# Long convolution: a GpSimd fold moved ahead of a low part, and two magnitude tiles added before the column sum

## The chip, the cores and the metric

One core of one Trainium2 chip (trn2) runs the whole program. The metric is device time in microseconds of that core; what is given is the median of three runs, and one more execution was profiled. Inputs, outputs and all arithmetic are fp32; most matmuls run on fp32r pairs, a high part and a low part.

## The reference, cut to what matters

The program is two blocks of a language model, one after the other. The change lies in the first mixer of the first block, a long convolution over T = 528 positions and E = 2048 channels. Its filters come from a small network, are weighted by a decay, and are divided by the sum of their magnitudes:

```python
filt = (hdn @ w4.astype(F32)).reshape(T, 2, D_INNER)
filt = filt * jnp.exp(-t * deltas[None, :])[:, None, :]
filt = filt / (jnp.sum(jnp.abs(filt), axis=(0, 1), keepdims=True) + HY_FILTER_EPS)
...
y = jnp.fft.irfft(jnp.fft.rfft(vf, n=n, axis=1) * jnp.fft.rfft(taps, n=n, axis=0)[None], n=n, axis=1)[:, :T]
return (y + vf * skip.astype(F32)).astype(v.dtype)
```

What the change touches is the sum of magnitudes over positions, one number for each channel, and the order of work around it.

## The kernel before, in words

The five engines (TensorE, ScalarE, VectorE, GpSimd, called POOL, and SyncE) each run a program written out by hand, and wait for each other by counters ("cv.pe", "cv.vec", "cv.act", "cv.pool"). Nothing is planned by a scheduler: the order on each engine is the order in the functions `tensor_conv`, `scalar_conv`, `vector_conv`, `gpsimd_conv` and `sync_conv`.

The 2048 channels are cut into 8 chunks c of 256, each two halves h of 128. The Fourier transforms are matmuls with tables. Positions are folded first (sum and difference of a position and its mirror), which leaves 265 rows in three tiles: 128, 128 and 9 (the 9 repeated, 41 partitions). Frequencies come in five groups z: two even, two odd, and a rest. In chunk c, each group z goes like this:

- TensorE: `tensor_freq` part 0, the transform of the signal (14 passes), then `tensor_filter`, a step of the filter network's last layer for chunk c+1, then `tensor_freq` part 1, the transform of the filter. Behind group 1 it transposes the folded signal of chunk c+1, half 0, and behind group 3 half 1 (`tensor_turned`, L1095, six transposes, three for each of two folds m).
- ScalarE: `scalar_freq` evicts the filter's part (hc), `scalar_filter` takes magnitudes for chunk c+1, `scalar_product` rounds the product's high part into Y_h.
- VectorE: `vector_filter` multiplies taps and decay into hp (L1007), `vector_differ` forms sums and differences into fsum (L1023, two instructions), `vector_freq` multiplies signal and filter (L1196, from PSUM) and forms real and imaginary parts rr (L1202, L1203). `vector_larger` (L1029) takes the larger of two magnitudes: with a = forward plus backward and b = forward minus backward, |forward| + |backward| = max(|a|, |b|), so the tile dec[:, i] then holds magnitudes, for i in the three tiles of positions and s in two parts of 256 channels.
- POOL: `gpsimd_freq` makes the low part Y_l of the product (L103). Behind group 1 of chunk c it folds half 1 of chunk c+1 (`gpsimd_fold`: for each of two folds m an add or subtract of 128x263 at L1077 and two small copies at L1078 and L1080). Behind groups 0 and 1 it also makes the low part of the finished output y of chunk c-1 (`gpsimd_out`). Behind group 4 come the low part of the next weights (`gpsimd_w4`), the fold of half 0 for chunk c+2, and two products of gate and signal (`gpsimd_back`, L1275).

Then TensorE transforms back (`tensor_back`, 48 passes; `tensor_back_end`, L1231, 8 passes, which wait for POOL's low part of group 4), and `tensor_filter_end` (L1056) sums the magnitudes of chunk c+1 over positions: for each half h six matmuls with one column on the moving side, dec as the weights, against ones, or against wf[:, 6] (2 in partition 0, 1 elsewhere, since position 0 stands in halved) for the first tile, or against wf[:, 5] (1 for the nine true rows) for the third. The hardware runs an fp32 matmul of this kind as two passes, so the 12 matmuls are 24 passes of LDWEIGHTS and MATMUL. VectorE reads the sums (`vector_filter_end`), adds 1e-6 and takes the reciprocal rn, which scales the output of chunk c+1 at its end.

Behind the mark "norm" of `tensor_filter_end`, SyncE loads the next chunk's decay into dec (`sync_conv`). After "norm" TensorE starts chunk c+1 with `tensor_freq`, whose bank must be free of VectorE's read y0 (`vector_back`, L1259 and L1260, first half).

In chunk 0 part of this work stands ahead, inside the projections of the mixer: POOL issues the tables' loads (L1443 to L1445), makes the low part of the weights of chunk 1 (`gpsimd_w4(e, w, 1)`), waits for the projections to be over (`hyena_over`), issues one more table and folds half 0 of chunk 1. TensorE runs `tensor_filter_end` for chunk 0 after the signal's transform of groups 0 and 1. Chunk 7 has no filter work.

Of the kernel before, what the change touches and what calls it, by code (L numbers as in the profile page):

```python
# [6 lines left out]
F32 = mybir.dt.float32  # L7
# [3 lines left out]
ALU = mybir.AluOpType  # L11
# [129 lines left out]
def build(nc, stack, I, C, out):  # L141
# [3 lines left out]
    def sb(name, shape, dt, at):  # L145
        return nc.alloc_sbuf_tensor_at(name, shape, dt, offset=at, align_bytes=16)
# [220 lines left out]
    HT = at  # L367
# [209 lines left out]
    def sync_norm0(e, w):  # L577
# [14 lines left out]
                      for j, n in enumerate("hl"))  # L592
    wf = sb("wf", [128, 7], F32, HT + 16704)
    w4r = sb("w4r", [128, 2, 256], F32, PH2)
# [436 lines left out]
    def scalar_filter(e, w, c, step):  # L1031
# [14 lines left out]
        act(e, abs0[0:n], hp[0:n, 0, :], ACT.Abs).then_inc(*mark("cv.act", "abs0", c, i))  # L1046

    def tensor_filter_end(e, w, c):
        w.wait_ge("cv.vec", "vT", c, 0)
        w.wait_ge("wf")  # L1050
        once, first_ = wf[:, 5:6], wf[:, 6:7]
        for h in range(2):
            for i in range(3):
                w.wait_ge("cv.vec", "ab", c, i)
                for s in range(2):
                    t = e.matmul(vb[0][:, h:h + 1], lhsT=dec[:, i, s, 128 * h:128 * h + 128], rhs=once if i == 2 else first_ if i + s == 0 else ones[:, 0:1],  # L1056
                                 start=(i == 0 and s == 0), stop=(i == 2 and s == 1))
        t.then_inc(*mark("cv.pe", "norm", c))
# [367 lines left out]
    def gpsimd_conv(e, w):  # L1426
# [17 lines left out]
        e.dma_start(flat(lf[0][:]), C["lf"][0]).then_inc(*land("mats2"))  # L1444
        e.dma_start(lb_x[:], C["lb"]).then_inc(*land("mats2"))  # L1445
        gpsimd_w4(e, w, 1)
        hyena_over(w)
# [5 lines left out]
        for c in range(8):  # L1453
            for z in range(5):
                gpsimd_freq(e, w, c, z)
                if c < 7 and z == 1:
                    gpsimd_fold(e, w, c + 1, 1)
                if c and z < 2:
                    gpsimd_out(e, w, c - 1, z)
            if c < 6:  # L1460
                gpsimd_w4(e, w, c + 2)
                gpsimd_fold(e, w, c + 2, 0)
            if c < 7:
                gpsimd_back(e, w, c, 0)
                gpsimd_back(e, w, c, 1)
# [2885 lines left out]
def constants():  # L4351
# [26 lines left out]
    co[264] = 0  # L4378
    wf = np.full((128, 7), 2 / 1056, np.float32)
    wf[:, 5] = np.arange(128) < 9  # L4380
    wf[:, 6] = 1
    wf[0, 6] = 2
    wf[0, 0] = 1 / 1056
# [81 lines left out]
```

## Time and profile before

| | |
|---|---|
| median of three runs | 2385.81 us (2380.79 to 2391.12) |
| profiled execution, its own time | 2386.13 us |
| its span | 2384.2 us |
| busy in the span: TensorE / its weight loads | 2226.8 us (93%) / 1848.7 us (78%) |
| VectorE / ScalarE / POOL | 1365.9 (57%) / 1002.5 (42%) / 623.7 (26%) |
| mean granted TensorE clock | 0.969 of full speed |
| the convolution's main loop | about 416 to 704 us of the span |

Times on the traces are microseconds from the span's start. The profiled execution's own time is the span and 1.9 us around it. A timeline row gives start, length, engine, line, operation, the tile written and the tiles read; "x2" means that two like instructions are merged, and their length is from the first's start to the last's end. In brackets stands the idle time before it and what ended it. An instruction's length on VectorE and POOL includes the time for which it was issued and stood still. The lines L99, L103 and L115 are helpers (high part, low part, activation), so tiles tell them apart.

### The profile page before, as it was taken

Reading aid. Unit: us, or ns where it says so; the run is one execution under the profiler, and the core shown is the slowest. Engines: PE = TensorE matmul, PEld = TensorE weight load, DVE = VectorE, ACT = ScalarE, POOL = GpSimd, SP = SyncE. Lnnn points to the kernel's source line nnn. Section 1 sums busy time; section 2 is a strip of 40 time slices with the busy share of each in tenths; the row PEclk is TensorE's granted clock in tenths of the full one; section 3 lists DMA queues with packets and bytes.
Section 4 is the critical chain, followed back from the end, with each engine's and each line's share of the span. In section 5 each row is a group of like instructions: output and inputs, shape, how many; then the busy total and the mean of one; then the engine's idle time right before and its main releaser. Section 6 shows DMA issues by size and latency. Waiting matters only on the chain.

```text
span 2384.2 us, 36903 instructions
## 1 busy us (share of the span) xinstructions
PE 2226.8 (93%) x15305; PEld 1848.7 (78%) x15305; DVE 1365.9 (57%) x2335; ACT 1002.5 (42%) x1824; POOL 623.7 (26%) x520
## 2 busy tenths in 40 slices
PE   7999999999999899999999989889989999699997
PEld 7999999899999888999999967856776677333332
DVE  4455545898863566667666666789455664411112
ACT  4434434444442455655656552435424432211112
POOL 1111123555631122322322201203220111133331
PEclk9999999999999999999999989999988999799999
DMA  5322332210033222322222224312331143799993
GB/s 183 96 82 89 93 114 64 72 36 19 32 104 95 72 64 73 82 69 72 80 68 75 54 53 118 89 36 76 95 106 49 32 146 98 291 363 374 375 374 145
DMA packets 228641, 274.78 MB, mean 115 GB/s; under 512 B 41448, under 2 KB 193993, under 8 KB 215930
## 3 DMA queue, kind: packets, MB, share of 16 engines
q1 hardware_dynamic: 212634, 256.68, 33.7%
q0 software_dynamic: 15264, 13.65, 1.8%
q8 instruction: 121, 1.98, 0.3%
q10 hardware_dynamic: 576, 2.10, 0.2%
q14 instruction: 46, 0.38, 0.0%
HBM read 305.18 MB, written 23.13 MB: 138 GB/s over the span
## 4 chain that ended last, share of the span: by engine, by line
PE 69%; DVE 15%; ACT 8%; issue 3%; POOL 2%; DMA 1%; SPq 0%; ACTq 0%; POOLq 0%; DVEq 0%
PE ps L93 15%; PE ps L94 15%; PE ps L95 15%; PE ps L4065 7%; PE ps L4108 4%; ACT sp L115 2%; ACT whi L99 2%; DVE wlo L103 2%; PE ps L1876 2%; PE ps L4035 1%; DVE p L2174 1%; PE ps L3181 1%; PE ps L3126 1%; PE ps L1056 1%; PE ps L3048 1%
## 5 line engine op out<-in xcount | busy, mean ns | idle before, releaser
L93 PE MATMUL ps<-hn_h,whi 128*128 128x264 f32 (+2 forms) x2256 | 688.9, 305 | 27.2 <-DVE wlo L103 8.5
L94 PE MATMUL ps<-hn_l,whi 128*128 128x264 f32 (+2 forms) x2256 | 670.4, 297 | 0.0
L95 PE MATMUL ps<-hn_h,wlo 128*128 128x264 f32 (+2 forms) x2256 | 670.3, 297 | 0.0
L93 PEld LDWEIGHTS ps<-hn_h,whi 128*128 128x128 f32 x2256 | 429.6, 190 | 52.7 <-issue 19.2
L94 PEld LDWEIGHTS ps<-hn_l,whi 128*128 128x128 f32 x2256 | 430.1, 191 | 9.6 <-issue 0.2
L95 PEld LDWEIGHTS ps<-hn_h,wlo 128*128 128x128 f32 x2256 | 428.6, 190 | 11.5
L103 POOL TENSOR_TENSOR wlo<-wraw,whi 128x2048 fp32r<-128x2048 f32 (+1 forms) x44 | 158.4, 3601 | 465.8 <-ACT whi L99 465.8
L99 ACT ACTIVATE whi<-wraw 128x2048 fp32r<-128x2048 f32 (+1 forms) x134 | 202.4, 1511 | 44.1 <-PE ps L95 37.9
L103 DVE TENSOR_TENSOR wlo<-wraw,whi 128x2048 fp32r<-128x2048 f32 (+1 forms) x90 | 172.0, 1911 | 50.4 <-ACT whi L99 50.2
L4065 PE MATMUL ps<-ex_raw,xT 128*64 128x512 f32 x600 | 135.4, 595 | 0.0
L766 DVE SCALAR_TENSOR_TENSOR c<-ub,vec,c 128x528 f32<-128x528 f32 x48 | 45.5, 948 | 123.3 <-ACT c L115 123.3
L4079 DVE SCALAR_TENSOR_TENSOR gt<-gt,ps 128x256 f32<-128x256 f32 x24 | 10.1, 421 | 171.4 <-ACT gt L115 171.4
L4065 PEld LDWEIGHTS ps<-ex_raw,xT 128*64 128x64 f32 x600 | 42.0, 137 | 76.4 <-issue 74.2
L115 ACT ACTIVATE ub<-ps,vec 128x528 f32<-128x528 f32 x48 | 33.7, 702 | 143.0 <-PE ps L95 143.0
L115 ACT ACTIVATE p<-ps,stat 128x528 f32<-128x528 f32 x64 | 45.0, 703 | 106.4 <-DVE stat L2160 106.4
L4108 PE MATMUL ps<-ex_raw,aT 128*64 128x512 f32 x312 | 87.6, 598 | 0.5 <-ACT aT L115 0.5
L2160 DVE TENSOR_REDUCE stat<-ps 128x1 f32<-128x528 f32 x128 | 84.0, 697 | 2.3 <-PE ps L1876 1.3
L115 ACT ACTIVATE gt<-ps 128x256 f32<-128x256 f32 x24 | 9.2, 384 | 161.3 <-PE ps L4065 161.3
L93 PE MATMUL ps<-yh,whi 128*128 128x272 f32 (+1 forms) x256 | 73.8, 288 | 2.4 <-POOL yl L103 2.4
L94 PE MATMUL ps<-yl,whi 128*128 128x272 f32 (+1 forms) x256 | 73.5, 287 | 0.0
L95 PE MATMUL ps<-yh,wlo 128*128 128x272 f32 (+1 forms) x256 | 73.4, 287 | 0.0
L2174 DVE SCALAR_TENSOR_TENSOR p<-p,stat,sp 128x528 f32<-128x528 f32 x60 | 46.1, 768 | 47.5 <-ACT sp L115 47.5
(703 smaller groups left out, 5296.8 us busy)
## 6 DMA issues: line engine op xcount, KB each, us to landing
ex_raw<-in_w_gate_up SPq DMA_DIRECT2D x49, 1024.0 KB, 7.8
wraw<-in_hy_w_in SPq DMA_DIRECT2D x32, 1024.0 KB, 5.7
wraw<-in_da_w_in SPq DMA_DIRECT2D x64, 512.0 KB, 4.2
ex_raw<-in_w_down SPq DMA_DIRECT2D x26, 1024.0 KB, 7.7
wraw<-in_w_gate_up SPq DMA_DIRECT2D x15, 1024.0 KB, 7.6
wraw<-in_w_in SPq DMA_DIRECT2D x14, 1024.0 KB, 5.4
wraw<-in_hy_w_out SPq DMA_DIRECT2D x8, 1024.0 KB, 7.6
wraw<-in_da_w_out SPq DMA_DIRECT2D x8, 1024.0 KB, 7.7
```

The lines of the kernel that those rows point to most:

```text
L93: e.matmul(out, lhsT=l[0], rhs=r[0], start=start, stop=False)
L94: e.matmul(out, lhsT=l[0], rhs=r[1], start=False, stop=False)
L95: return e.matmul(out, lhsT=l[1], rhs=r[0], start=False, stop=stop)
L99: return e.activation(hi, src, ACT.Copy, bias=0.0, scale=scale)
L103: return e.tensor_tensor(lo, src, hi.bitcast(F32), ALU.subtract)
L115: return e.activation(out, in_, func, bias=bias, scale=scale, accum_out=accum)
L766: e.scalar_tensor_tensor(cc[:], u[:, 0:T], V["conv_w0"][:, q:q + 1], cc[:], ALU.mult, ALU.add).then_inc(*mark("hy.vec", "tap", x))
L1876: t = e.matmul(sc[m][:, y, 0:264], lhsT=qk[l][c, q], rhs=qk[r][c, ks], start=(l + r == 0), stop=(l == 1))
L2160: e.tensor_reduce(mx[:, m:m + 1], sc[m][:, :, 0:264], AX.XY, ALU.max, negate=True).then_inc(*mark("da.vec", "max", h, i, m))
L2174: e.scalar_tensor_tensor(p[0][:], p[0][:], ls[:, 0:1], p[1][:], ALU.mult, ALU.add).then_inc(*mark("da.vec", "p", h, i))
L4065: t = e.matmul(bank[2 + n % 2][half, :], lhsT=xT[n % 2][:, 4 * g + k, half], rhs=unsplit(c)[:, k, :], start=(g == 0 and k == 0), stop=(g = ...
L4108: t = e.matmul(bank[6 + g][half, :], lhsT=aT[n % 2][:, k, half], rhs=unsplit(c)[:, k, 512 * g:512 * g + 512], start=(k == 0), stop=(k == 1))
```

## The change

Three things change. POOL folds half 1 of chunk c+1 ahead of the low part of group 1 instead of behind it; the low part of y stays behind. POOL adds the first magnitude tile onto the second (128x512) and then the second's two channel parts together (128x256), in a new function `gpsimd_total`, which stands ahead of the low part of group 4 for chunk c+1, and for chunk 0 behind the tables' loads. And `tensor_filter_end` runs, for each half, four matmuls for six: the sum tile against ones, one partition (position 0) once more against one, which takes the place of the weight 2, and the two of the third tile. These are 16 passes for 24. It now waits for POOL's total and for the last maximum before its first pass. The column wf[:, 6] goes.

```diff
+    def gpsimd_total(e, w, c):
+
+        w.wait_ge("cv.vec", "ab", c, 1)
+        a, b = (dec[:, i].rearrange("p s c -> p (s c)") for i in range(2))
+        e.tensor_tensor(b, b, a, ALU.add).then_inc(*mark("cv.pool", "both", c))
+        w.wait_ge("cv.pool", "both", c)
+        e.tensor_tensor(dec[:, 1, 0], dec[:, 1, 0], dec[:, 1, 1], ALU.add).then_inc(*mark("cv.pool", "total", c))
+
     def tensor_filter_end(e, w, c):
         w.wait_ge("cv.vec", "vT", c, 0)
         w.wait_ge("wf")
-        once, first_ = wf[:, 5:6], wf[:, 6:7]
+        once = wf[:, 5:6]
+        w.wait_ge("cv.pool", "total", c)
+        w.wait_ge("cv.vec", "ab", c, 2)
         for h in range(2):
-            for i in range(3):
-                w.wait_ge("cv.vec", "ab", c, i)
-                for s in range(2):
-                    t = e.matmul(vb[0][:, h:h + 1], lhsT=dec[:, i, s, 128 * h:128 * h + 128], rhs=once if i == 2 else first_ if i + s == 0 else ones[:, 0:1],
-                                 start=(i == 0 and s == 0), stop=(i == 2 and s == 1))
+            out, cols = vb[0][:, h:h + 1], slice(128 * h, 128 * h + 128)
+            e.matmul(out, lhsT=dec[:, 1, 0, cols], rhs=ones[:, 0:1], start=True, stop=False)
+            e.matmul(out, lhsT=dec[0:1, 0, 0, cols], rhs=ones[0:1, 0:1], start=False, stop=False)
+            for s in range(2):
+                t = e.matmul(out, lhsT=dec[:, 2, s, cols], rhs=once, start=False, stop=s == 1)
         t.then_inc(*mark("cv.pe", "norm", c))
...
         e.dma_start(lb_x[:], C["lb"]).then_inc(*land("mats2"))
+        gpsimd_total(e, w, 0)
         gpsimd_w4(e, w, 1)
         hyena_over(w)
...
         for c in range(8):
             for z in range(5):
-                gpsimd_freq(e, w, c, z)
                 if c < 7 and z == 1:
                     gpsimd_fold(e, w, c + 1, 1)
+                if c < 7 and z == 4:
+                    gpsimd_total(e, w, c + 1)
+                gpsimd_freq(e, w, c, z)
                 if c and z < 2:
                     gpsimd_out(e, w, c - 1, z)
```

## Rows read from the trace of the kernel before

**Rows 1.** Busy by stretch: length, PE, PEld, DVE, ACT, POOL busy, clock, DMA share, GB/s.
```profile
450.00:485.00 35.00, 32.95 (x275) 32.24 (x273) 32.27 (x48) 16.84 (x28) 21.10 (x22) 1.00 0.10 31
```

**Rows 2.** Chain of waits in order of time: start, length, what.
```profile
416.15 2.59 PE ps L1056 x24
...
450.30 2.57 PE ps L1056 x24
...
519.90 2.57 PE ps L1056 x24
...
555.78 3.01 PE ps L1056 x24
...
593.22 2.90 PE ps L1056 x24
...
666.56 2.57 PE ps L1056 x24
```

**Rows 3.** Waits, 415 to 705 us: total us, times, longest.
```profile
PEld ps L1095 <- POOL fold L1080: 10.8, 7, 1.6
...
PE ps L1095 <- POOL fold L1080: 9.0, 7, 1.4
```

**Rows 4.** Timelines, TensorE and weight load, chunk 1: start, length, engine, line, operation.
```profile
469.87 0.54 PE L1095 MATMUL ps<-ident,fold 128*128 128x128 f32 x3
...
471.79 0.29 PEld L1095 LDWEIGHTS ps<-ident,fold 128*128 128x128 f32 x3 [1.64 <-POOL fold L1080]
```

**Rows 5.** Timeline of VectorE, chunk 1.
```profile
457.53 1.23 DVE L1196 TENSOR_TENSOR prods<-ps,hc 128x1024 f32<-128x1024 f32 x1 [0.20 <-ACT hc L115]
...
461.04 3.41 DVE L1023 TENSOR_TENSOR fsum<-hp 128x512 f32<-128x512 f32 x2
...
465.62 0.42 DVE L1202 TENSOR_TENSOR rr<-prods 128x256 f32<-128x256 f32 x1
...
468.92 0.50 DVE L1202 TENSOR_TENSOR rr<-prods 128x256 f32<-128x256 f32 x1
...
470.38 1.29 DVE L1023 TENSOR_TENSOR fsum<-hp 128x512 f32<-128x512 f32 x2
472.84 0.68 DVE L1007 TENSOR_TENSOR hp<-ps,dec 41x512 f32<-41x512 f32 x1 [1.17 <-PE ps L988]
...
475.37 0.69 DVE L1029 TENSOR_TENSOR dec<-dec,sq 128x512 f32<-128x512 f32 x1
...
477.54 1.29 DVE L1023 TENSOR_TENSOR fsum<-hp 41x512 f32<-41x512 f32 x2
```

**Rows 6.** Timeline of GpSimd (POOL), chunk 1.
```profile
460.70 1.47 POOL L103 TENSOR_TENSOR Y_l<-rr,Y_h 128x512 fp32r<-128x512 f32 x1 [1.36 <-ACT Y_h L99]
462.12 1.78 POOL L103 TENSOR_TENSOR yl<-gg,yh 128x528 fp32r<-128x528 f32 x1
...
468.38 0.76 POOL L1077 TENSOR_TENSOR fold<-vv 128x263 f32<-128x263 f32 x1
...
471.69 1.31 POOL L103 TENSOR_TENSOR yl<-gg,yh 128x528 fp32r<-128x528 f32 x1
472.97 1.29 POOL L103 TENSOR_TENSOR Y_l<-rr,Y_h 128x512 fp32r<-128x512 f32 x1
476.19 1.29 POOL L103 TENSOR_TENSOR Y_l<-rr,Y_h 128x512 fp32r<-128x512 f32 x1 [1.93 <-ACT Y_h L99]
481.68 1.29 POOL L103 TENSOR_TENSOR Y_h<-rr,Y_h 17x512 fp32r<-17x512 f32 x1 [4.19 <-ACT Y_h L99]
```

**Rows 7.** Timeline of ScalarE, chunk 1.
```profile
469.78 0.63 ACT L99 ACTIVATE Y_h<-rr 128x512 fp32r<-128x512 f32 x1 [1.53 <-DVE rr L1203]
```

**Rows 8.** Timelines of GpSimd and VectorE, chunk 0.
```profile
414.32 0.57 POOL L1445 DMA_DIRECT2D lb_x<-c_lb  x1
...
423.00 0.69 DVE L1007 TENSOR_TENSOR hp<-ps,dec 128x512 f32<-128x512 f32 x1 [0.96 <-DMA dec<-c_dec]
```

**Rows 9.** Busy by stretch, behind the passes at 519.90.
```profile
523.00:527.00 4.00, 4.00 (x24) 4.00 (x23) 3.88 (x7) 0.00 (x0) 3.88 (x7) 0.58 0.75 228
```

More of the change, by code:

```diff
@@ L592, in build @@
                       for j, n in enumerate("hl"))
-    wf = sb("wf", [128, 7], F32, HT + 16704)
+    wf = sb("wf", [128, 6], F32, HT + 16704)
     w4r = sb("w4r", [128, 2, 256], F32, PH2)
@@ L4378, in constants @@
     co[264] = 0
-    wf = np.full((128, 7), 2 / 1056, np.float32)
+    wf = np.full((128, 6), 2 / 1056, np.float32)
     wf[:, 5] = np.arange(128) < 9
-    wf[:, 6] = 1
-    wf[0, 6] = 2
     wf[0, 0] = 1 / 1056
```

## The prediction

> **What bounds the kernel now.** I read busy time by stretch first. In the stretch that holds chunk 1 of the convolution, TensorE is busy 32.95 of 35 us and VectorE 32.27, so two engines are almost full and neither can be shortened alone [rows 1]. GpSimd has 21.10 us of work. Next the chain of waits in order of time, for its marks: the 24 passes that sum the magnitudes start at 450.30, 519.90, 555.78, 593.22 and 666.56 us (the blocks near 485.1 and 630.7 are not shown), so chunks 1 and 2 take 69.60 us, 34.8 each, chunk 3 35.88, chunk 4 37.44, and the six periods 216.26 together, 7.46 more than six of 34.8 [rows 2]. The extra lies in chunks 3 to 6, at the lower clock, below. Then who waits for whom: TensorE and its weight load wait for the fold's last copy in seven chunks, 9.0 and 10.8 us in all [rows 3]. The timelines of TensorE and of its weight load show it once: three transposes at 469.87, and the weight load for the next three at 471.79, idle 1.64 us before it until the fold ended [rows 4].
>
> **The change, TensorE's part.** Per chunk 24 passes become 16. The 24 take 2.57 us, 0.107 us a pass [rows 2]. Eight fewer: 0.86 us a chunk. Four of the sixteen read one partition of dec; no row has such a pass. From below I bound it by nothing, from above by 0.107 us; I take 0.107, since they load the same 128 columns. The range that this leaves is 0.43 us a chunk, 3 us in all. The Trainium skill ("TensorE: Matmul & The Clock Gate", section "LDWEIGHTS (loading the stationary operand)") says that a load costs by its columns and not by the rows in contraction, which is also 0.107 here; no run here shows it. With the fold ahead of the low part of group one, the 1.64 us go as well: POOL ends the first low part of y at 463.90, what the fold waits for (the transposes of the first half, ahead of group two) is over by then, and two adds of 0.75 with four small copies end near 467.7, two us before TensorE asks [rows 4, 6]. Together TensorE could run 2.5 us a chunk faster, if nothing else stopped it.
>
> **VectorE's part.** It gets back what it waited for TensorE: 1.17 us before hp at 472.84, and 0.20 us before the products at 457.53 [rows 5]. That is 1.37 us a chunk; with this alone its period is 33.4 us, over TensorE's 32.3. So VectorE sets the pace, and what delays VectorE counts in full.
>
> **What delays VectorE.** Two sums of L1023 take 1.29 us for the pair at 470.38, but 3.41 us at 461.04 [rows 5]. In the second case POOL ran a low part (460.70 to 462.17) and another (462.12 to 463.90, 1.78 us where the same kind took 1.31 at 471.69) [rows 6]. The times fit a strict alternation: the sum waits for POOL's instruction, POOL's next waits for the sum, and so on, 2.1 us lost for VectorE. The product at 457.53 reads PSUM and takes 1.23 us; such instructions I count as free of it. So the position of every POOL instruction against VectorE's SBUF-only ones is a cost, and the change moves or adds ten of them a chunk (six of the fold, two low parts, two adds). By place:
> (a) The fold's adds now fall on 464 to 467, with the real and imaginary parts of group one (465.62, one of the two of 0.42) [rows 5]. At most one 0.75 us add stands in the way; I take 0.3, least 0.
> (b) The second low part of y (1.31 us) leaves 471.69, where VectorE idled, and follows Y_l of group one at about 468.5 to 469.8, onto the real part at 468.92 [rows 5, 6]. Between 0 and 1.3; I take 0.5, where the add there now costs 0.08 (0.50 for 0.42).
> (c) Y_l of group two waits for folds until 472.97 now, though ScalarE wrote its high part at 469.78 to 470.41 [rows 6, 7]. It will start at once, between the two sums of L1023 at 470.38. Between 0 and 1.29; I take 1.05, the middle of the pattern at 461.04.
> (d) The new adds: 128x512, priced by the low part of the same shape (1.29 us), and 128x256, priced by the fold's add of 128x263 (0.76 us, 468.38) [rows 6]. They stand behind Y_l of group three, which ends at 477.48, and its input (the maximum, done at 476.06) is there. VectorE starts two sums at 477.54 [rows 5]. 0.06 us decides who is first. Between 0 and 2.04; I take 1.3, the first add in the way and the second partly.
> Sum (a) to (d): 3.15, less 1.37 is +1.8 us a chunk. The Trainium skill ("SBUF — State Buffer", section "SBUF: two separate sides") states this as a rule: GpSimd and a VectorE instruction with two SBUF inputs hold one shared pair of ports for a whole instruction and the other side blocks fully. By that, the sum would be the same; the 3.41 us pair agrees with it.
> Behind (d) the cost is not hidden: the last group's products, ScalarE's high part, POOL's low part of group four and TensorE's eight passes of L1231 follow in a chain, and before the change that low part is ready at 482.97, 1.1 us ahead of them (they take the last 1.0 us before the block at 485.1) [rows 6].
>
> **The queues.** total for chunk c+1 stands ahead of the low part of group four, which arrives 4.19 us after POOL went idle [rows 6]; that gap holds the 2.0 us. The 16 passes wait for total, done near 481, against 485 when TensorE arrives: nothing. SyncE's loads of the next dec wait for the passes, which are no later: nothing. For chunk 0 it is otherwise: total(0) comes behind the last table's load (414.32, done issuing at 414.89) [rows 8], takes 2.0 to 2.1, so until 417.0; the passes that started at 416.15 start then and end at 418.8 for 418.7 [rows 2]. The dec load behind them, for which VectorE waits 0.96 us at 423.00 [rows 8], slips with it, and the w4 low part on POOL moves to 418.3, still before TensorE. +0.1 us.
>
> **The clock.** The mean granted clock is 0.58 from 523 to 527 us, part of it at the lower level, 1.2 GHz for 2.4 [rows 9], and before that TensorE had run the one-column passes (from 519.90, 2.57 us). Chunk 3 loses 35.88 - 34.8 = 1.1 us by it and chunk 4 2.6 [rows 2]; chunks 5 and 6 share the other 3.7. The passes' block shrinks by a third, which speaks for fewer such stretches. But where VectorE sets the pace, TensorE will stand idle right behind them, for the bank that VectorE's back part reads last (y0). By my estimate 1.1 us: 0.86 from the shorter block and some 0.7 of the slack of the low part above, less 0.5 that y0 is ahead now. Passes and wait together are 2.8 us for 2.6 before. I take the clock as unchanged, and the loss of such chunks as +1.4 instead of +1.8, since in them VectorE waits for the products' input anyway (part of the 0.86 us comes back).
>
> **Sum.** Chunk 0: +0.1 and +0.9 (no low part of y there, so no (b)); chunks 1 and 2: 2 x 1.8; 3 to 6: 4 x 1.4; chunk 7 has no filter work: 0. That is 10.2 us on the profiled execution's 2386.1 us, whose span is 2384.2; the median of three runs is 2385.8, so 2396.0. After the convolution the engines follow in series, and I let the delay through whole. A measurement of this kernel can tell about 0.5% (12 us) from no change, so +10.2 itself lies within it.
>
> **Rivals.** (1) Faster: the alternation decides nothing, since POOL's instructions slip into gaps where VectorE reads PSUM. Then VectorE's 1.37 us a chunk (9.6 in seven) is gained, and if the shorter block also ends the low-clock stretches, up to 7.5 more: 2386 - 9.6 = 2376, at best 2369. It decides from the point where (a) to (d) cost under 1.37 us a chunk. For it: VectorE has 2.7 us idle a chunk. Against: the pair at 461.04. (2) The clock turns against it: each block, now with a wait behind it, is followed by a low stretch, as chunks 4 and 5 are now (2.6 us); three chunks that have none or a short one add 1.5 to 2.6 each, some 8 us more: 2404. For it: TensorE idles more. Against: the passes themselves are fewer. (3) A draw: (a) and (b) cost nothing and (c) and (d) 1.4 us together, as much as VectorE gets back: 2386. For it: every one of (a) to (d) has nothing as its lower end. Against: all four would have to come out low by half.
>
> **Chances.** Forecast 0.60 (own range 2390 to 2402), faster 0.16, clock 0.13, draw 0.11. The range 2376 to 2405 reaches from rival (1) to rival (2). Slower by over 0.5%: a third of the forecast's case and most of rival (2), 0.31. Faster by over 0.5%: a third of rival (1), 0.06. Within: 0.63.
>
> **What would show it.** Right: the fold's wait gone from the list and the transposes in one run of six; periods between blocks near 36.5; VectorE's sums at about 470 and 478 each near 2.4 us or more a pair instead of 1.29; TensorE waiting behind the 16 passes for VectorE's back part; 16 passes in 1.7 us. Wrong: periods near 33.4 with the pairs still 1.29, or low-clock stretches gone.

## The result, and the profile after

The changed kernel takes 2402.4 us (median of 6 runs, 2398.7 to 2405.2) where the kernel before, in the same runs, takes 2387.0 (6 runs, 2380.8 to 2391.7): a ratio of 1.0069, 95% interval 1.0054 to 1.0084. It is slower by 0.7%, or 15.4 us. The forecast was 10.2 us slower, with 2376 to 2405 as its range. The sign and the range held; the size is half as large again, and the outcome fell to the side of "slower by over 0.5%", which had been given 0.31 against 0.63 for "within 0.5%".

The profiled execution took 2404.15 us, span 2402.4. By the starts of the one-column passes (418.04, 453.33, 491.27, 529.18, 566.93, 606.13, 644.07 and 682.08 us) its periods are 35.29, 37.94, 37.91, 37.75, 39.20, 37.94 and 38.01. Before they were 34.15, 34.79, 34.80, 35.89, 37.43, 37.44 and 35.90, from a first start at 415.99 to an eighth at 666.39 [rows 2]. So the eighth block comes 15.7 us later: 2.05 at the first start, 1.14 in chunk 0, 6.3 in chunks 1 and 2, 6.2 in chunks 3 to 6. What follows the eighth block is as long as before within 2.4 us (1722.1 for 1719.7, own time less start).

Busy time by stretch, after: the periods of chunks 1 and 2, then the first 8 us behind the start of two blocks (length, PE, PEld, DVE, ACT, POOL busy, granted clock, DMA share, GB/s).
```profile
453.33:491.27 37.94, 34.26 (x265) 32.96 (x263) 35.23 (x48) 16.42 (x28) 23.81 (x24) 0.96 0.09 29
491.27:529.18 37.91, 34.21 (x264) 32.90 (x263) 35.23 (x48) 16.42 (x28) 23.79 (x24) 0.95 0.09 29
...
491.37:499.37 8.00, 7.31 (x48) 7.17 (x47) 7.67 (x12) 1.47 (x4) 6.82 (x8) 0.79 0.41 131
...
567.03:575.03 8.00, 7.31 (x41) 7.17 (x40) 7.67 (x12) 1.47 (x4) 6.81 (x8) 0.64 0.40 131
```
The same view before, behind the starts at 484.93, 519.73 and 555.62:
```profile
485.03:493.03 8.00, 8.00 (x71) 8.00 (x70) 7.70 (x13) 2.43 (x6) 7.20 (x9) 1.00 0.44 133
519.83:527.83 8.00, 8.00 (x58) 8.00 (x57) 7.01 (x12) 1.09 (x3) 7.20 (x9) 0.79 0.44 130
555.72:563.72 8.00, 8.00 (x49) 8.00 (x48) 7.08 (x12) 1.09 (x3) 7.20 (x9) 0.63 0.37 111
```
VectorE has the same 48 instructions in a period, but they are busy 35.23 us for some 32.1: "busy" holds the time in which an instruction stood still against one of POOL. Since both instructions then count as busy, a block by the other engine never shows as idle time. TensorE's busy time didn't fall either, though it has fewer passes, because part of each period now runs at the lower clock (e2 below has both kinds: 32.59 us busy in its period at the full clock, 34.14 in one with a low stretch). The mean granted clock behind a block was 1.00 twice, 0.79 twice and 0.63 twice in six periods before; after, it is 0.79 five times and 0.64 once. No period after the change is free of it.

Waits after, 410 to 725 us (total us, times, longest):
```profile
...
PE ps L987 <- DVE hp L1007: 10.8, 19, 1.0
...
PE ps L93 <- DVE prods L1206: 9.7, 14, 1.2
...
PE ps L93 <- DVE sq L1270: 4.3, 7, 0.7
```
The wait for the fold [rows 3] is gone, as meant. In its place TensorE waits for VectorE at three places: filters (L987, for hp), products (L93, for prods) and y0 (L93, for L1270). Before, the first two were 1.8 and 2.0 us in all. The 9.0 us it had waited for POOL became slack in an engine that is not the last.

VectorE in chunk 2, after (a period with a low stretch; start, length, line, operation, idle before). The letters of the prediction are (a) 508.11, (b) 511.80, (c) 513.82, (d) 521.05.
```profile
500.45 1.23 DVE L1206 TENSOR_TENSOR prods<-ps,hc 128x1024 f32<-128x1024 f32 x1 [1.30 <-ACT hc L115]
501.71 0.42 DVE L1212 TENSOR_TENSOR rr<-prods 128x256 f32<-128x256 f32 x1
...
503.56 3.39 DVE L1023 TENSOR_TENSOR fsum<-hp 128x512 f32<-128x512 f32 x2
...
508.11 0.81 DVE L1212 TENSOR_TENSOR rr<-prods 128x256 f32<-128x256 f32 x1
...
511.80 1.06 DVE L1212 TENSOR_TENSOR rr<-prods 128x256 f32<-128x256 f32 x1
...
513.82 2.40 DVE L1023 TENSOR_TENSOR fsum<-hp 128x512 f32<-128x512 f32 x2
516.35 0.68 DVE L1007 TENSOR_TENSOR hp<-ps,dec 41x512 f32<-41x512 f32 x1
...
521.05 2.89 DVE L1023 TENSOR_TENSOR fsum<-hp 41x512 f32<-41x512 f32 x2
```
POOL beside it:
```profile
507.90 0.74 POOL L1087 TENSOR_TENSOR fold<-vv 128x263 f32<-128x263 f32 x1
...
511.24 1.33 POOL L103 TENSOR_TENSOR yl<-gg,yh 128x528 fp32r<-128x528 f32 x1
...
513.93 1.74 POOL L103 TENSOR_TENSOR Y_l<-rr,Y_h 128x512 fp32r<-128x512 f32 x1 [1.35 <-ACT Y_h L99]
...
520.96 1.29 POOL L1052 TENSOR_TENSOR dec<-dec 128x512 f32<-128x512 f32 x1
522.32 1.06 POOL L1054 TENSOR_TENSOR dec<-dec 128x256 f32<-128x256 f32 x1
```
Read the two by their ends. (a): the fold's second add runs 507.90 to 508.64, and the real part issued at 508.11 ends at 508.92. (b): the low part of y runs 511.24 to 512.57; the real part issued at 511.80 needs 0.42 and ends at 512.86, shortly behind it. (c): POOL's low part, issued 0.11 us behind the pair of sums, takes 1.74 for 1.29 and ends at 515.67, the pair at 516.22. (d): the pair of sums is issued at 521.05, 0.09 us behind the first add, and ends at 523.94, behind the second add (523.38); both adds are over before the pair is. The second add in turn takes 1.06, for 0.74 where nothing stood against it (in e7, chunk 0). Taken against their lengths before [rows 5] the four places cost VectorE 0.39, 0.56, 1.11 and 1.60 us: 3.66, for 3.15 forecast. The instructions that read PSUM are as long as before whatever POOL does: between the second and the eighth block the products take 1.20 to 1.23 us and hp 0.67 to 0.69 in each of the fourteen profiled kernels. The Trainium skill ("SBUF — State Buffer", section "SBUF: two separate sides") gives this as an exclusive lock for a whole instruction between GpSimd and a VectorE instruction with two SBUF inputs; the rows agree.

### The profile page after: what moved, and what is told of

It reads as the page before. It is cut to its first block, busy times and chain, and to the rows that moved or that the text cites. A ratio compares the mean times of both kernels' runs of the same rounds, so it can differ in the third digit from the quotient of the medians.

```text
span 2402.4 us, 36799 instructions
## 1 busy us (share of the span) xinstructions
PE 2233.3 (93%) x15241; PEld 1848.9 (77%) x15241; DVE 1394.4 (58%) x2335; ACT 1001.5 (42%) x1824; POOL 645.0 (27%) x536
## 4 chain that ended last, share of the span: by engine, by line
PE 64%; DVE 21%; ACT 9%; issue 4%; DMA 1%; POOL 1%; SPq 0%; ACTq 0%; DVEq 0%; POOLq 0%
PE ps L93 14%; PE ps L94 13%; PE ps L95 13%; PE ps L4078 7%; PE ps L4121 4%; DVE fsum L1023 2%; DVE prods L1206 2%; ACT sp L115 2%; DVE wlo L103 2%; PE ps L1889 1%; ACT whi L99 1%; PE ps L4048 1%; PE ps L3194 1%; DVE p L2187 1%; DVE work L2791 1%
## 5 line engine op out<-in xcount | busy, mean ns | idle before, releaser
L93 PE MATMUL ps<-hn_h,whi 128*128 128x264 f32 (+2 forms) x2256 | 688.0, 305 | 26.4 <-DVE wlo L103 7.5
L93 PEld LDWEIGHTS ps<-hn_h,whi 128*128 128x128 f32 x2256 | 428.5, 190 | 51.9 <-issue 18.0
L115 ACT ACTIVATE ub<-ps,vec 128x528 f32<-128x528 f32 x48 | 33.7, 702 | 143.0 <-PE ps L95 143.0
L93 PE MATMUL ps<-yh,whi 128*128 128x272 f32 (+1 forms) x256 | 73.8, 288 | 2.4 <-POOL yl L103 2.4
```

The costliest lines, as they stand in the source:

```text
L93: e.matmul(out, lhsT=l[0], rhs=r[0], start=start, stop=False)
L115: return e.activation(out, in_, func, bias=bias, scale=scale, accum_out=accum)
```

## The experiments

Block 8 below is the start of the eighth block. A period is called full where the 8 us behind its block show a granted clock of 1.00, low where they show 0.79. "Low of 6" counts the periods of chunks 1 to 6 below 1.00. All of it is from one profiled execution of each, so the last column can differ in another execution.

| kernel | ratio (95%) | median us | block 8 | full | low | low of 6 |
|---|---|---|---|---|---|---|
| before | 1 | 2384 to 2387 | 666.39 | 34.8 | 35.9 | 4 |
| the change | 1.0069 (1.0054-1.0084) | 2402.4 | 682.08 | none | 37.75-38.0 | 6 |
| e1 fold early only | 0.9990 (0.9975-1.0004) | 2384.7 | 666.03 | 35.64 | 36.35 | 3 |
| e2 adds and 16 passes | 1.0020 (1.0005-1.0035) | 2390.8 | 673.31 | 36.20 | 36.9 | 5 |
| e3 16 passes only | 0.9969 (0.9954-0.9983) | 2379.3 | 659.45 | 34.80 | 35.49 | 1 |
| e4 adds, 24 passes | 1.0022 (1.0008-1.0036) | 2392.0 | 672.27 | 36.2 | 36.9 | 4 |
| e5 POOL moved away | 0.9991 (0.9974-1.0008) | 2385.4 | 665.73 | 35.08 | 35.7 | 5 |
| e6 only the adds moved | 1.0023 (1.0011-1.0035) | 2392.1 | 673.65 | 36.30 | 37.0 | 5 |
| e7 e5, first adds earlier | 0.9987 (0.9977-0.9996) | 2385.4 | 664.15 | 35.08 | 35.7 | 5 |
| e8 e7, full-height passes | 1.0000 (0.9988-1.0013) | 2387.0 | 661.84 | 35.1 | 35.75 | 4 |
| e9 before, POOL moved | 0.9965 (0.9951-0.9979) | 2379.8 | 658.81 | 34.1-34.4 | 35.15 | 4 |
| e10 e9, first pair too | 0.9933 (0.9917-0.9949) | 2368.8 | 649.16 | 32.2-32.8 | 33.7 | 4 |
| e11 e8, one add | 0.9972 (0.9958-0.9987) | 2377.7 | 657.86 | 34.56 | 35.28 | 3 |
| e12 e11, first pair too | 0.9965 (0.9952-0.9978) | 2377.8 | 653.73 | 33.4-34.1 | 34.62 | 1 |

Block 8 and the median don't rank every pair alike: what follows block 8, edited by none of these but for the places of y's low parts in chunk 7 (e5 and e7 to e12), took (to the end of the execution's own time) between 1717 and 1726 us in the fourteen profiled executions. The periods judge a mechanism; the ratio judges a kernel.

**e1: the fold alone is moved.** From the kernel before:
```diff
             for z in range(5):
-                gpsimd_freq(e, w, c, z)
                 if c < 7 and z == 1:
                     gpsimd_fold(e, w, c + 1, 1)
+                gpsimd_freq(e, w, c, z)
```


> The kernel before with nothing but the fold of half 1 ahead of group one's low part; 24 passes, no adds on POOL. Theory A (POOL and VectorE take turns, so the position of POOL's instructions decides): the fold's wait goes and VectorE gets 1.37 us a chunk back, but the real part of group one takes 0.81 instead of 0.42, that of group two 1.06 instead of 0.50, and the sums of L1023 behind group three's filter 2.40 instead of 1.29, as after the change. Net +0.7 us a chunk, chunk 1 near 35.5 us, median +5 us. Rival B (the two new adds make the whole loss, the fold's new place is a gain): chunk 1 near 33.4 to 34.0 us, median -6 to -9 us.

VectorE of e1, chunk 2:
```profile
502.35 0.81 DVE L1202 TENSOR_TENSOR rr<-prods 128x256 f32<-128x256 f32 x1
...
506.03 1.07 DVE L1202 TENSOR_TENSOR rr<-prods 128x256 f32<-128x256 f32 x1
...
508.07 2.39 DVE L1023 TENSOR_TENSOR fsum<-hp 128x512 f32<-128x512 f32 x2
...
515.30 1.29 DVE L1023 TENSOR_TENSOR fsum<-hp 41x512 f32<-41x512 f32 x2
```
(a), (b) and (c) are there at their lengths after the change, (d) is not. At the full clock the period is 35.64, 0.84 more than before: taking a wait away made the period longer. By busy time of the first such period (450.05 to 485.69, against 450.14 to 484.93 before) VectorE is busy 34.26 us for 32.06 and idle 1.38 for 2.73. So the idle time came back as forecast (1.35 for 1.37: 1.04 before hp, 0.20 before the products, 0.11 ahead of the last group's), and 2.20 us went. (a), (b) and (c) are 2.06 by their lengths (lengths overlap a little, so they add up to more than the busy time). The fourth place is one that neither the prediction nor the expectation names, group zero's real part. Before (chunk 1), then e1 with POOL's product of gate and signal beside it:
```profile
458.79 0.84 DVE L1202 TENSOR_TENSOR rr<-prods 128x256 f32<-128x256 f32 x1
```
```profile
458.88 1.14 DVE L1202 TENSOR_TENSOR rr<-prods 128x256 f32<-128x256 f32 x1
...
457.10 2.63 POOL L1275 TENSOR_TENSOR gg<-gg,vv 128x528 f32<-128x528 f32 x2
```
VectorE no longer waits the 0.20 us ahead of the products, so it comes to the real part earlier in POOL's work, which is at L1275 until 459.73 (459.34 before), and stands there for what it had gained.

In the median nothing of the 0.84 is left (ratio 0.999; 5 us slower had been expected): three periods are low instead of four, none reached 37.4 us, and the six together are 215.99 us for 216.25. So the move costs what the steps say, and in this execution the clock gave it back.

**e2: the adds and the 16 passes, the fold late.** From the changed kernel:
```diff
-                if c < 7 and z == 1:
-                    gpsimd_fold(e, w, c + 1, 1)
                 if c < 7 and z == 4:
                     gpsimd_total(e, w, c + 1)
                 gpsimd_freq(e, w, c, z)
+                if c < 7 and z == 1:
+                    gpsimd_fold(e, w, c + 1, 1)
```


> The changed kernel with the fold put back behind the low part: POOL's adds and 16 passes alone. Theory A: the fold's wait of 1.64 us stays, the sums at group four take 2.9 us instead of 1.29, chunk 0 loses 2.0 us before the passes; +1.4 us a chunk and +2.4 for chunk 0, median +12 us. Rival B: the same sums, but then this kernel alone carries all of the measured loss, +15 us or more. Rival C (the low-clock stretches behind the blocks make the loss, not the turns): +6 to +8 us, with the pair at group four unchanged.

```profile
511.16 1.29 DVE L1023 TENSOR_TENSOR fsum<-hp 128x512 f32<-128x512 f32 x2
...
513.62 0.68 DVE L1007 TENSOR_TENSOR hp<-ps,dec 41x512 f32<-41x512 f32 x1 [1.17 <-PE ps L988]
...
518.31 2.88 DVE L1023 TENSOR_TENSOR fsum<-hp 41x512 f32<-41x512 f32 x2
```
These lines of VectorE's timeline in e2 are the mirror of e1: (c) is back at 1.29 with the wait of 1.17 behind it, (d) is 2.88. Full-clock period 36.20, so +1.40. The whole came to 5.2 us where 12 had been expected. Block 8 is 6.9 us later, 4.5 of it in the six periods, though six times 1.40 are 8.4: the low stretches cost these six 3.5 us (220.71 less six of 36.20), for 7.46 before.

**e3: the 16 passes without the adds.** From the changed kernel; of the first magnitude tile only one position enters the sum, and of the second only one of its two parts; the rest is left out:
```diff
-        w.wait_ge("cv.pool", "total", c)
+        w.wait_ge("cv.vec", "ab", c, 1)
         w.wait_ge("cv.vec", "ab", c, 2)
...
-        gpsimd_total(e, w, 0)
...
-                if c < 7 and z == 4:
-                    gpsimd_total(e, w, c + 1)
```
(and the fold late, as before).


> The kernel before with 16 passes for 24, and nothing on POOL: the second tile is summed alone, the first tile's sum is left out but for position 0, so the channel sums are too small. Theory A: TensorE's block takes 2.0 us instead of 2.57; VectorE waited only 0.20 us there, so -0.2 us a chunk at the full clock, and fewer low-clock stretches give back up to 7 us: median -1 to -8 us, the sums of L1023 as before. Rival C: the shorter block changes nothing in the clock, -1 us.

The full-clock period is 34.80, to the hundredth what it was: the eight passes are worth nothing there. VectorE sets the pace, and the one wait for TensorE that a shorter block could take from it, 0.20 us before the products, is gone; but its real part of group zero now stands longer against POOL, 1.13 for 0.84:
```profile
458.32 1.13 DVE L1212 TENSOR_TENSOR rr<-prods 128x256 f32<-128x256 f32 x1
```
Yet the kernel is 0.3% faster and block 8 comes 6.9 us earlier. Of these, 6.8 us lie in the six periods, and all of that is clock: one low period for four. (One of its ten runs took 3101.2 us; the other nine are 2376 to 2383.) Whether the shorter block is what brought this is not shown: e2 has the same 16 passes and five low periods.

**e4: the adds with the 24 passes.** From the kernel before, with the function gpsimd_total and its two calls as in the change; the second magnitude tile then counts the first once more:
```diff
+        w.wait_ge("cv.pool", "total", c)
         for h in range(2):
             for i in range(3):
...
+        gpsimd_total(e, w, 0)
...
+                if c < 7 and z == 4:
+                    gpsimd_total(e, w, c + 1)
                 gpsimd_freq(e, w, c, z)
```


> The kernel before with POOL's two adds ahead of group four's low part, whose total the 24 passes wait for; they sum it together with the first tile, so the channel sums are too large. Theory A: the same collision as with 16 passes, the pair of L1023 at group four 2.9 us instead of 1.29: +1.6 us a chunk, chunk 0 +2.0, median +13 us. If instead the passes' form (one partition, ones) is what costs, this one is near 0.

36.2 full and 36.9 low, the same as e2: with the adds in, 24 passes or 16 make no difference, and the ratios (1.0022, 1.0020) agree. Its 6.3 us are half of the 13 expected, as in e2 and for the same reason (its low stretches cost 2.7 us in the six periods). The price is that of the adds on POOL, and nothing of it is paid back by TensorE.

**e5: POOL's instructions moved under VectorE's PSUM-reading ones.** From the changed kernel. Nothing is taken out; POOL gets two waits, and the second low part of y goes behind group two:
```diff
     def gpsimd_total(e, w, c):
         w.wait_ge("cv.vec", "ab", c, 1)
+        if c:
+            w.wait_ge("cv.vec", "sum", c, 2)
...
+                if c < 7 and z == 2:
+                    w.wait_ge("cv.vec", "sum", c + 1, 1)
                 gpsimd_freq(e, w, c, z)
-                if c and z < 2:
-                    gpsimd_out(e, w, c - 1, z)
+                if c and z in (0, 2):
+                    gpsimd_out(e, w, c - 1, z // 2)
```


> The changed kernel with POOL's instructions moved off VectorE's SBUF-only ones by two waits and one move: total waits for the sums of group four, group two's low part waits for the sums behind group three's filter, and the second low part of y goes behind group two's. Theory A (turns decide): the pairs of L1023 are back at 1.29 us, the period falls from 36.9 us at full clock to 34.0 to 34.5, and with it most waits of TensorE; from norm block to norm block 34.0 to 35.5 with low stretches, chunk 0 still +2 to +3 us. Median 2382 to 2390, 12 to 20 us below the changed kernel. If the turns were not the cause, it stays within 4 us of the changed kernel's 2402.

VectorE of e5, chunk 2:
```profile
509.58 1.29 DVE L1023 TENSOR_TENSOR fsum<-hp 128x512 f32<-128x512 f32 x2
...
512.85 0.96 DVE L1214 TENSOR_TENSOR rr<-prods 128x256 f32<-128x256 f32 x1
...
516.24 1.29 DVE L1023 TENSOR_TENSOR fsum<-hp 41x512 f32<-41x512 f32 x2
...
519.17 0.95 DVE L1215 TENSOR_TENSOR rr<-prods 57x256 f32<-57x256 f32 x1
```
and POOL's first add, held for 1.49 us until the sums are over:
```profile
517.67 1.29 POOL L1054 TENSOR_TENSOR dec<-dec 128x512 f32<-128x512 f32 x1 [1.49 <-DVE fsum L1023]
```
Both pairs are 1.29 again, by two waits and one changed place, with POOL's work unchanged. The kernel is 17 us faster than the changed one and equal to the one before. The full-clock period is 35.08, above the 34.0 to 34.5 expected. (a) is still there (0.81 for 0.42), group zero's real part takes 1.13 as in e1, and there are two new collisions of 0.55 (0.96 for 0.42 at L1214, 0.95 for 0.41 at L1215): the pairs are free, so POOL's instructions now reach into the real and imaginary parts. Of all runs this is the one that shows the mechanism, since no work, no buffer and no engine changed, only the order and the starts on POOL.

**e6: the adds alone are held** (the first half of e5's edit).


> The changed kernel with only total made to wait for the sums of group four. Theory A: the pair at group four goes from 2.89 to 1.29 us, the real part behind it may take 0.4 more; 1.2 us a chunk less, median 8 us below the changed kernel's, near 2394, with the pair behind group three's filter still 2.40. A rival in which POOL's total is needed early (TensorE waits for it): the 16 passes start later and the time does not fall.

The pair at the end of the chunk is back at 1.29, the one in (c) stays at 2.38, and a part is caught (0.95 at L1215). A low period is 37.0 for 37.9, so 0.9 of (d)'s 1.6 us can be had by that wait alone.

**e7: chunk 0's adds ahead of the tables' loads.** From e5:
```diff
         e.dma_start(tl_x[:], C["tl"]).then_inc(*land("mats0"))
+        gpsimd_total(e, w, 0)
         w.wait_ge("w.done", HEAD)
...
-        gpsimd_total(e, w, 0)
         gpsimd_w4(e, w, 1)
```


> As the kernel that moves POOL's instructions out of the way, and total of chunk 0 stands where POOL waits for the projections, before the tables' loads: the weights' sums of L958 take 0.43 us again instead of 1.94, the first block starts at 416.0 to 416.5 instead of 418.0, 1.5 to 2.5 us less than without it. Median 2380 to 2387. If instead the block's start is set by the last maximum on VectorE and not by the turns, it still starts near 418.

After the change, VectorE, POOL and TensorE in chunk 0:
```profile
414.49 1.94 DVE L958 TENSOR_TENSOR w4s<-w4r 128x256 f32<-128x256 f32 x1
416.36 0.94 DVE L959 TENSOR_TENSOR w4s<-w4r 128x256 f32<-128x256 f32 x1
...
414.80 1.34 POOL L1052 TENSOR_TENSOR dec<-dec 128x512 f32<-128x512 f32 x1
416.22 0.80 POOL L1054 TENSOR_TENSOR dec<-dec 128x256 f32<-128x256 f32 x1
...
418.04 0.35 PE L1064 MATMUL ps<-ones,dec 128*128 128x1 f32 x2 [1.96 <-DVE dec L1029]
```
In e7:
```profile
414.52 0.43 DVE L958 TENSOR_TENSOR w4s<-w4r 128x256 f32<-128x256 f32 x1
414.86 0.42 DVE L959 TENSOR_TENSOR w4s<-w4r 128x256 f32<-128x256 f32 x1
```
The add of 1.34 us stood against L958, which should take 0.43 and took 1.94; behind L958 and L959 comes chunk 0's last maximum (L1029), for which the passes wait 1.96 us. With the adds out of there the first block starts at 416.02 for 417.70 in e5 and block 8 comes 1.6 us earlier. The median shows none of it (2385.4 both).

**e8: the passes with one partition made full height.** From e7, with a seventh column of wf that holds a one in partition 0 alone:
```diff
-            e.matmul(out, lhsT=dec[0:1, 0, 0, cols], rhs=ones[0:1, 0:1], start=False, stop=False)
+            e.matmul(out, lhsT=dec[:, 0, 0, cols], rhs=wf[:, 6:7], start=False, stop=False)
```


> As the kernel with total of chunk 0 early, but the pass over one partition becomes a pass over all 128, against a column that is 1 in partition 0 and 0 elsewhere. After the change two passes over one partition take 0.30 us where two others take 0.21. Theory: the block falls from 2.04 to 1.71 us, 0.3 us a chunk on TensorE and 0 to 0.3 on the time, and low-clock stretches become no more: median 0 to 4 us lower than 2385.4. Rival: the price is the switch of the column and not the single partition; the block stays at 2.04.

TensorE's passes after the change (the next instruction, y0's, waits 0.69):
```profile
491.27 0.28 PE L1064 MATMUL ps<-ones,dec 128*128 128x1 f32 x2
491.48 0.38 PE L1065 MATMUL ps<-ones,dec 1*128 1x1 f32 x2
491.78 0.60 PE L1067 MATMUL ps<-wf,dec 128*128 128x1 f32 x4
...
494.14 0.58 PE L93 MATMUL ps<-vT_h,mats_h 128*128 128x256 f32 x1 [0.69 <-DVE sq L1270]
```
In e8:
```profile
483.77 0.35 PE L1066 MATMUL ps<-ones,dec 128*128 128x1 f32 x2
483.98 0.36 PE L1067 MATMUL ps<-wf,dec 128*128 128x1 f32 x2
484.21 0.58 PE L1069 MATMUL ps<-wf,dec 128*128 128x1 f32 x4
```
From the start of a pair to the start of what follows it is 0.30 us with one partition (491.48 to 491.78) and 0.23 with 128 (483.98 to 484.21). The block of 16 takes 1.8 us for 2.05, so the rival (the price is the switch of the column) is out: the column is still switched. The time stays where it was (ratio 1.000; 0 to 4 us less had been expected): TensorE waits longer for y0 instead (7.1 us in all for 4.5).

**e9: the kernel before, POOL moved.** 24 passes, no adds; the fold early, and group two's low part and the second low part of y as in e5:
```diff
-                gpsimd_freq(e, w, c, z)
                 if c < 7 and z == 1:
                     gpsimd_fold(e, w, c + 1, 1)
-                if c and z < 2:
-                    gpsimd_out(e, w, c - 1, z)
+                if c < 7 and z == 2:
+                    w.wait_ge("cv.vec", "sum", c + 1, 1)
+                gpsimd_freq(e, w, c, z)
+                if c and z in (0, 2):
+                    gpsimd_out(e, w, c - 1, z // 2)
```


> The kernel before with 24 passes and no adds, the fold early, and the two low parts moved off VectorE's sums as in the other kernel. Theory A: the 1.37 us a chunk that VectorE waited come back less 0.4 for the real part of group one: full-clock periods 33.6 to 34.0, against 35.6 with the fold early alone; median 2372 to 2380. If VectorE's wait is only moved, periods stay at 34.8.

0.35% faster than before. The move of the fold is worth having once what it pushes is put where VectorE reads PSUM: 35.64 in e1 becomes 34.1 to 34.4 (33.6 to 34.0 had been expected). The pair in group two's place is 1.29, the first one still 3.40.

**e10: the first pair too.** From e9:
```diff
-                if c < 7 and z == 2:
-                    w.wait_ge("cv.vec", "sum", c + 1, 1)
+                if c < 7 and z in (0, 2):
+                    w.wait_ge("cv.vec", "sum", c + 1, z // 2)
+                if z == 4:
+                    if c < 7:
+                        w.wait_ge("cv.vec", "sum", c + 1, 2)
+                    if c:
+                        gpsimd_out(e, w, c - 1, 1)
                 gpsimd_freq(e, w, c, z)
-                if c and z in (0, 2):
-                    gpsimd_out(e, w, c - 1, z // 2)
+                if c and z == 2:
+                    gpsimd_out(e, w, c - 1, 0)
```


> 24 passes, no adds, the fold early and clear of VectorE's sums as before, and now group zero's low part waits for the first pair of L1023, which takes 3.4 us in every kernel so far; the two low parts of y go behind group two and ahead of group four. Theory A: this pair falls to 1.3 us, full-clock periods from 33.9 to about 32.6, where TensorE's own work ends the gain (34.8 less the fold's 1.64 and the waits for products of 0.6); median 2368 to 2375. If VectorE does not set the pace any more in the kernel with the fold clear, or the low parts only collide elsewhere, the median stays at 2379 or over.

VectorE's first pair in e10, and the POOL instruction that is held behind it:
```profile
493.89 1.29 DVE L1023 TENSOR_TENSOR fsum<-hp 128x512 f32<-128x512 f32 x2
```
```profile
495.26 1.30 POOL L103 TENSOR_TENSOR Y_l<-rr,Y_h 128x512 fp32r<-128x512 f32 x1 [3.81 <-DVE fsum L1023]
```
Busy time of the period of chunk 2 in e10:
```profile
481.48:515.33 33.85, 33.62 (x273) 33.52 (x272) 31.09 (x48) 16.67 (x28) 20.43 (x22) 0.95 0.10 32
```
This beats both kernels: 2368.8 us, ratio 0.9933 (0.9917 to 0.9949) to the one before and 1.4% under the changed one (2368.8 / 2402.4, each median from its own runs). The pair that had cost 3.41 us [rows 5] is 1.29. TensorE is busy 33.62 of 33.85 us (and 32.18 of 32.22 in the period before, at the full clock), VectorE 31.09: TensorE now sets the pace, while POOL waits up to 3.81 us.

**e11: one add and 20 passes.** From e8:
```diff
         e.tensor_tensor(b, b, a, ALU.add).then_inc(*mark("cv.pool", "both", c))
-        w.wait_ge("cv.pool", "both", c)
-        e.tensor_tensor(dec[:, 1, 0], dec[:, 1, 0], dec[:, 1, 1], ALU.add).then_inc(*mark("cv.pool", "total", c))
...
-            e.matmul(out, lhsT=dec[:, 1, 0, cols], rhs=ones[:, 0:1], start=True, stop=False)
+            for s in range(2):
+                e.matmul(out, lhsT=dec[:, 1, s, cols], rhs=ones[:, 0:1], start=s == 0, stop=False)
```


> As the one-hot kernel, with one add on POOL a chunk (128x512, behind the sums of group four, beside a product that reads PSUM) and 20 passes instead of two adds and 16. Theory A: the real and imaginary parts of group four take 0.42 each again instead of 0.55 and 0.95, 0.7 us a chunk less on VectorE, 0.4 more on TensorE's block: full-clock periods 33.8 to 34.2, median 2379 to 2383, about as the kernel with the fold clear and 24 passes.

The second add's place costs 0.5 us a period (34.56 for 35.08 full, 35.28 for 35.75 low; one of the three low periods is 34.56 too), which fits the 0.54 of e5 at L1215 (the same instruction, L1214 there, is 0.41 in e11). It had saved four passes that are worth nothing at the full clock. Ratio 0.9972; the full-clock period had been expected at 33.8 to 34.2, the median at 2379 to 2383.

**e12: e11 with the first pair freed** (group zero's low part held for its sum, the first low part of y behind group two, the second ahead of group three's).


> The two best together: group zero's low part behind the first pair of L1023, one add on POOL and 20 passes with the one-hot column; the second low part of y stands ahead of group three's low part, where it can meet the real parts or the maximum (0 to 1 us). Theory A: full-clock periods 32.2 to 33.0 against 32.2 with 24 passes and no add, and fewer low-clock stretches behind the shorter block, which cost that kernel 1.5 us in most chunks: median 2362 to 2369. If TensorE's block of 24 is not what calls the low stretches, or the second low part collides in full, the median is 2369 to 2374.

```profile
507.15 1.54 DVE L1214 TENSOR_TENSOR rr<-prods 128x256 f32<-128x256 f32 x1
```
Behind that line of VectorE stands this one of POOL:
```profile
505.62 2.79 POOL L103 TENSOR_TENSOR yl<-gg,yh 128x528 fp32r<-128x528 f32 x2
```
2362 to 2369 us had been expected; it took 2377.8, no better than e11. All three pairs are 1.29, but two low parts of y now stand in a row ahead of group three's and meet its imaginary part: 1.54 for 0.41. Full-clock periods had been expected at 32.2 to 33.0; one is 33.4 and four are 34.1, for 34.56 in e11. In the profiled executions the 4.1 us at block 8 are lost again behind it (1717.1 us in e11, 1721.0 in e12), where the two kernels differ only in the places of y's low parts in chunk 7; why, and why none of it is in the median, is not settled.

## Why the prediction was half right

**The mechanism held.** That VectorE sets the pace and that TensorE's 2.5 us a chunk would be slack is shown from both sides: e3 removes eight passes and the full-clock period stays at 34.80 (the little that VectorE gained by it went back to POOL), e4 puts them back under the adds and it stays at 36.2. That POOL's place costs VectorE time is shown by e5, where POOL's order and waits alone give 17 us back. The parts add up: 34.80 + 0.84 (e1) + 1.40 (e2) = 37.04. Both parts hold the same small gain of 0.18 us ahead of the last group's products (from the start of the second sum to theirs it is 0.79 us before and 0.61 in e1; VectorE's wait of 0.11 is gone), which counts once: 37.22. With 0.7 for the lower clock (36.35 - 35.64 in e1, 35.49 - 34.80 in e3, 36.9 - 36.2 in e2) it is 37.92, where the change shows 37.91 to 38.01 four times and 37.75 once.

**Sizes at the full clock.** The forecast was +1.8 a chunk; by e1 and e2 it is +2.42 (an estimate, since the change has no period at the full clock). Of the places, (a) took 0.39 for 0.3, (b) 0.56 for 0.5, (c) 1.11 for 1.05 and (d) 1.60 for 1.3; the largest miss is (d), where 0.06 us in the order decided. The other miss is a place that the prediction left out: it counted the 0.20 us before the products as gained, and group zero's real part took it back (1.14 in e1, 1.12 in e2, 1.13 in e3, for 0.84). Over six periods the 0.62 makes 3.7 us.

**The step that failed first is chunk 0.** The forecast had +0.1 at the block and +0.9 behind; it came to +2.05 and +1.14. The step followed total(0) down the queues (loads, w4's low part) and not against VectorE: the same rule that priced (a) to (d) was not applied to L958 and L959, and the last maximum stands behind those. e7 takes 1.7 of the 2.05 away by the place of the adds alone. That is 2.2 of the 5.5 us missed at block 8.

**The clock, taken as unchanged.** Its direction was wrong and its sum nearly right. Every period has a low stretch now, as rival (2) said: the 8 us behind a block are at 0.79 where they had been 1.00. But a low stretch costs 0.7 us in e1 to e3, and 1.1 (or 2.6 at 0.63) in the kernel before. The rows show why it is not the full delay. At the lower clock VectorE waits for group zero's products, at 0.79 for 1.3 us in e1, e2, e3 and the change (1.14 in the period of 37.75), and for 1.70 before (0.20 at the full clock); but POOL's L1275 is over by the time it gets to the real part, which then takes 0.42 or 0.43. That holds in all 84 periods (fourteen kernels, six each): with no wait ahead of the products the real part takes 1.11 to 1.14, with one of 0.18 to 0.20 it takes 0.84 or 0.85, with one over 1 us 0.42 or 0.43. In e1 the products start 1.4 later and 0.72 comes back (1.14 to 0.42), in the kernel before they start 1.5 later and 0.42 comes back (0.84 to 0.42). So the 0.42 of the change's real part above is no gain over the kernel before, which has it too at the lower clock. Taking 37.22 as the full-clock period, the six lose 228.75 - 223.32 = 5.4 us to the clock, for 7.46 before. The forecast wanted 1.6 us of that to come back (four times 0.4) and got 2.0. With chunk 0 and the sizes that makes 2.2 + 3.7 - 0.4 = 5.5 us, and 10.2 becomes the 15.7 measured at block 8. The agreement of 15.7 there with 15.4 in the medians is in part luck: the profiled execution as a whole is 18.0 us longer, and what follows block 8 scatters by some us.

**TensorE behind the passes.** The 16 take 2.04 to 2.1 us, not 1.7: the four with one partition take 0.15 each, beyond the upper bound of 0.107 that I had set for them (with all 128 partitions in each the block is 1.8, e8). So the wait for y0 is 0.7 and not 1.1, as the block ends later. This moved no time (e8). The Trainium skill ("TensorE: Matmul & The Clock Gate", section "LDWEIGHTS (loading the stationary operand)") has a load cost by columns alone; 0.30 for a pair with one partition and 0.23 with 128 speak against that as a price of the whole pass, and the measurement decides.

**The rivals.** (1) decides where (a) to (d) cost under 1.37 us; they cost 3.66. Its end, 2376, is near where e9, e11 and e12 lie (2377.7 to 2379.8), and e10 is at its best case (2368.8 for 2369), so the gain was there to have, with another placement. (3) is out by the same sum. (2) named the right thing for the clock and the wrong price.

**What stays open.** e3 has one low stretch in six, e2 and e4, with 16 and 24 passes, five and four, e1 three, the kernel before four, all by one execution each. TensorE stands idle behind the block for y0 in e2 and the change (0.7 us each time) but not in the kernel before, e1 or e4, which have low stretches too; and e12, idle there up to 0.6 us, has one alone. Neither the block's length nor the idle time sorts these cases alone, and I didn't find what does. That e1's cost vanished from its median rests on this.

## What to carry to other kernels

Price work that is offloaded to GpSimd by what it blocks, not by how idle GpSimd is: list the main engine's instructions that read two SBUF operands, lay each GpSimd instruction against them, and do so at every place where the change issues one, the first chunk too. Where the second engine has slack, holding it by a wait until the main engine reads PSUM was worth more here than any work removed: e10 takes no work out of the kernel before, only moves and holds POOL's instructions by three waits, and is 0.67% faster. And when two engines are almost full, judge an edit by the period between two marks at equal clock before looking at the total.

## What the runs showed of the hardware that I had not expected

A one-column pass that contracts one partition took longer (0.15 us) than one that contracts 128 (0.107 to 0.115). The lower clock followed blocks of one-column passes although TensorE counts as busy throughout (8.00 of 8.00 us at a granted clock of 0.79 and 0.63, before), so a full busy column is no sign of a full clock. And removing a wait of 1.6 us from TensorE, alone, made its period at the full clock 0.84 us longer (e1). A wait of 0.20 us that VectorE lost came back as 0.3 us more of standing against GpSimd in every period at the full clock of e1, e2 and e3.
